# The second block's mixing stage: weight rounding, group sums and the first projection rows are put in another order

## The reference, cut to what matters

```python
y_f = _fourier_mix(zf, w_fourier[l])                       # 256 columns
q, k = _rope(zq, positions), _rope(zk, positions)
y_a = _window_attn(q, k, v, sink[l])                       # 8 heads of 64
y_m = _memory_attn(zm, km, vm)                             # 4 heads of 64
gg = g_grp[l]
y = jnp.concatenate([_rmsnorm(y_f, gg[:256]), _rmsnorm(y_a, gg[256:768]), _rmsnorm(y_m, gg[768:])], axis=-1) @ w_out[l]
x = x + _rmsnorm(y, g_post_mix[l])
```

## Time and profile before

| what | us |
|---|---|
| median of 3 runs | 1994.9 (1992.32 to 1998.2) |
| the profiled execution | 1989.49 |
| its span | 1987.6 |
| TensorE busy in it | 1834.7 (92%) |
| VectorE busy | 1252.5 (63%) |
| ScalarE busy | 850.6 (43%) |
| GpSimd busy | 302.4 (15%) |
| mean granted clock of TensorE | 0.972 of full |

### The profile page before, as it was taken

One profiled execution on the slowest core, in us unless ns is written; L12 is line 12 of the kernel. 1 busy time (PEld: TensorE's weight loads), 2 busy tenths in 40 slices (PEclk: granted clock), 3 DMA queues, 4 the chain that ended last, 5 costly groups with the idle time before them and its releaser, 6 DMA issues. The chain is left out here.

```text
span 1987.6 us, 42705 instructions
## 1 busy us (share of the span) xinstructions
PE 1834.7 (92%) x18268; PEld 1606.2 (81%) x18268; DVE 1252.5 (63%) x2177; ACT 850.6 (43%) x1561; POOL 302.4 (15%) x341
## 2 busy tenths in 40 slices
PE   7999868968999999999998899999889999889997
PEld 5787437858688888889877799999589999679997
DVE  4574886677656434534667778645768667677753
ACT  4321576363423212222436455533654355554332
POOL 0201206134140000013004101012040012030001
PEclk9999989979999999999999999999999999999998
DMA  9752940010523232323320455555045465226543
GB/s 326 210 175 85 311 135 3 15 53 2 170 85 106 85 106 85 106 85 94 119 64 1 152 168 175 186 191 170 1 150 190 143 196 174 82 86 194 188 156 99
DMA packets 248982, 254.69 MB, mean 128 GB/s; under 512 B 6914, under 2 KB 247186, under 8 KB 248690
## 3 DMA queue, kind: packets, MB, share of 16 engines
q1 hardware_dynamic: 239214, 242.86, 38.2%
q10 hardware_dynamic: 8740, 8.51, 1.3%
q0 software_dynamic: 864, 0.98, 0.3%
HBM read 251.29 MB, written 1.05 MB: 127 GB/s over the span
## 5 line engine op out<-in xcount | busy, mean ns | idle before, releaser
L578 DVE TENSOR_TENSOR RING_rounded<-RING,SC_rounded 128x1024 fp32r<-128x1024 f32 (+2 forms) x390 | 461.2, 1225 | 228.5 <-ACT SC_rounded L571 228.2
L598 PE MATMUL bank<-OT_rounded,SC_rounded 128*128 128x256 f32 (+1 forms) x1808 | 575.3, 318 | 15.5 <-DVE HT_rounded L1173 6.8
L600 PE MATMUL bank<-OT_rounded,RING_rounded 128*128 128x256 f32 (+1 forms) x1808 | 571.6, 316 | 0.0
L599 PE MATMUL bank<-HT_rounded,SC_rounded 128*128 128x256 f32 (+1 forms) x1808 | 570.3, 315 | 0.0
L571 ACT ACTIVATE SC_rounded<-RING 128x1024 fp32r<-128x1024 f32 (+2 forms) x390 | 373.8, 1009 | 331.5 <-DMA RING<-in_l_mlp_w 184.8
L598 PEld LDWEIGHTS bank<-OT_rounded,SC_rounded 128*128 128x128 f32 x1808 | 344.0, 190 | 44.7 <-issue 9.0
L600 PEld LDWEIGHTS bank<-OT_rounded,RING_rounded 128*128 128x128 f32 x1808 | 342.5, 189 | 23.8
L599 PEld LDWEIGHTS bank<-HT_rounded,SC_rounded 128*128 128x128 f32 x1808 | 342.3, 189 | 23.2
L598 PE MATMUL bank<-PT_rounded,SC_rounded 128*128 128x256 f32 (+1 forms) x896 | 277.4, 310 | 5.0 <-DVE RING_rounded L578 5.0
L600 PE MATMUL bank<-PT_rounded,RING_rounded 128*128 128x256 f32 (+1 forms) x896 | 277.5, 310 | 0.0
L599 PE MATMUL bank<-PT_rounded,SC_rounded 128*128 128x256 f32 (+1 forms) x896 | 277.1, 309 | 0.0
(11 more groups left out here) (573 smaller groups left out, 2782.4 us busy)
## 6 DMA issues: line engine op xcount, KB each, us to landing
RING<-in_l_mlp_w SPq DMA_DIRECT2D x64, 1024.0 KB, 5.3
RING<-in_w_ffn_in SPq DMA_DIRECT2D x44, 1024.0 KB, 5.1
RING<-in_l_mod_w SPq DMA_DIRECT2D x32, 1024.0 KB, 6.6
RING<-in_l_w_in SPq DMA_DIRECT2D x25, 1024.0 KB, 5.9
RING<-in_w_ffn_out SPq DMA_DIRECT2D x16, 768.0 KB, 4.8
RING<-in_w_in SPq DMA_DIRECT2D x10, 1024.0 KB, 5.3
RING<-in_w_ffn_out SPq DMA_DIRECT2D x16, 640.0 KB, 5.1
PT<-in_l_mod_w SPq DMA_DIRECT2D x8, 1024.0 KB, 10.1
```

Of the source, the lines that this page charges most:

```text
L578: net.nc.vector.tensor_tensor(low, whole, net.high4(s, m)[:, 0:self.w.kts[s], :].bitcast(F32), ALU.subtract).then_inc(self.split_ready, 1)
L598: net.nc.tensor.matmul(bank[:, tokens], high, x_high, start=start, stop=False)
L599: net.nc.tensor.matmul(bank[:, tokens], high, x_low, start=False, stop=False)
L600: return net.nc.tensor.matmul(bank[:, tokens], low, x_high, start=False, stop=stop)
```

## The change

On ScalarE the four high halves of slots 0 and 1 are now the first instructions of the stage. On VectorE the first low half comes ahead of the rotations' products, the other three behind them. TensorE sums groups 0 and 1 after pair 3's weighted values, in banks 0 and 1, and only group 2 behind the last pair; ScalarE takes roots 0 and 1 ahead of the last shares. VectorE scales tiles 0 and 1 before the last output, tiles 6 and 7 behind it, then makes four low halves, and only then scales by root 2. ScalarE's highs follow that: two before the last squares, two behind, then root 2, then four. Every instruction is kept; only order and two banks change. Line numbers are higher after the change, by 2 in ScalarE's part of the mixers, by 4 to 8 in VectorE's, and by up to some 25 further on.

```diff
-    def on_pe(self, pe):
+    def on_pe(self, pe, between={}):
...
             if pair:
                 weigh(pair - 1)
+            if pair in between:
+                between[pair]()
...
+            if u == self.N - 1:
+                share(self.N // 2 - 1)
             if u % 2 == 1 and u >= 5:
                 square(u // 2 - 2)
-        share(self.N // 2 - 1)
+        between[self.N]()
         square(self.N // 2 - 2)
         square(self.N // 2 - 1)
...
+        weights.low(dve, 0, 0)
         for n in range(4):
             part(n)
+        weights.low(dve, 0, 1)
+        for m in range(2):
+            weights.low(dve, 1, m)
         maxima(0)
...
-    group_banks = [net.ps[6][:, lats], net.ps[7][:, lats], net.ps[6][:, lats]]
+    group_banks = [net.ps[0][:, lats], net.ps[1][:, lats], net.ps[6][:, lats]]
...
+            def sum_first_groups():
+                pe.wait_ge(mixers.transform_taken, 6)
+                sum_group(0, 0)
+                sum_group(1, 1)
+
+            mixers.on_pe(pe, {4: sum_first_groups})
+            pe.wait_ge(mixers.out_taken, 5)
+            sum_group(2, 3)
+            pe.wait_ge(group_root, 2)
             rows_side_by_side(pe, out, 0, group_split, order)
...
-            mixers.on_act(act, {8: lambda: runner.highs(act, 0), 9: lambda: runner.highs(act, 1)})
-            for g in range(3):
-                root(g)
-            for n, t in enumerate(order):
-                act.wait_ge(group_scaled, n + 1)
-                act.activation(out.x.high[:, t], out.x.whole[:, t], ACT.Copy).then_inc(group_high, 1)
+            runner.highs(act, 0)
+            runner.highs(act, 1)
+            mixers.on_act(act, {10: first_roots, 12: lambda: high(0, 2)})
+            high(2, 2)
+            root(2)
+            high(4, 4)
...
-            mixers.on_dve(dve, link)
-            runner.lows(dve, 0)
-            mixers.last_outputs(dve)
-            runner.lows(dve, 1)
...
+            mixers.on_dve(dve, link, out)
+            scale(0)
+            scale(1)
+            mixers.last_outputs(dve)
+            scale(2)
+            scale(3)
+            for n in range(4):
+                low(n)
+            scale(4)
+            for n in range(4, KT):
+                if n + 1 < KT:
+                    scale(n + 1)
+                low(n)
```

More of the change, by code:

```diff
@@ L1867, in on_act, with on_dve @@
                 between[u]()
+            if u == self.N - 1:
+                share(self.N // 2 - 1)
             if u % 2 == 1 and u >= 5:
                 square(u // 2 - 2)
-        share(self.N // 2 - 1)
+        between[self.N]()
         square(self.N // 2 - 2)
         square(self.N // 2 - 1)
-    def on_dve(self, dve, link):
+    def on_dve(self, dve, link, weights):
         net, nc, mem = self.net, self.nc, self.mem
@@ L2021, in _, with sum_group @@
         def _(pe):
[L2022 to L2035, removed]
-                step.then_inc(group_summed, 1)
+            def sum_group(g, squared):
+                for n, t in enumerate(groups[g]):
+                    if g:
+                        pe.wait_ge(mixers.squared, squared + n)
+                    step = nc.tensor.matmul(group_banks[g], net.const(C_ONES), mixed.squares[t], start=(n == 0),
+                                            stop=(n == len(groups[g]) - 1))
+                step.then_inc(group_summed, 1)
+            def sum_first_groups():
[6 more added lines that the diff above has]
+            pe.wait_ge(group_root, 2)
             rows_side_by_side(pe, out, 0, group_split, order)
@@ L2075, in root, with high, first_roots @@
                 act.activation(group_roots[g], group_roots[g], ACT.Exp, scale=-0.5).then_inc(group_root, 1)
-            mixers.on_act(act, {8: lambda: runner.highs(act, 0), 9: lambda: runner.highs(act, 1)})
-            for g in range(3):
-                root(g)
-            for n, t in enumerate(order):
-                act.wait_ge(group_scaled, n + 1)
-                act.activation(out.x.high[:, t], out.x.whole[:, t], ACT.Copy).then_inc(group_high, 1)
+            def high(first, count):
+                for n in range(first, first + count):
+                    act.wait_ge(group_scaled, n + 1)
+                    act.activation(out.x.high[:, order[n]], out.x.whole[:, order[n]], ACT.Copy).then_inc(group_high, 1)
+            def first_roots():
+                root(0)
+                root(1)
+            runner.highs(act, 0)
[4 more added lines that the diff above has]
+            high(4, 4)
             for n, (part, q) in enumerate(runner.slots):
@@ L2143, in scale, with low @@
                                                ALU.mult, ALU.mult).then_inc(group_scaled, 1)
[L2145 to L2148, removed]
+            def low(n):
+                t = order[n]
                 dve.wait_ge(group_high, n + 1)
```

## The result

The changed kernel takes 1982.28 us, the median of five runs (1973.1 to 1985.16), against 1997.65 us for five runs of the kernel before (1992.32 to 1998.2). The ratio is 0.992, with a 95% interval of 0.9903 to 0.9937: faster, by 15.4 us between the medians. 1979.4 us with 15.5 us gained was forecast.

What follows compares the result with a forecast made beforehand. Bound: ScalarE's unrelated rounding, TensorE's half clock after it, then a serial chain from output to low half. Layer 0's 8.3 plus layer 1's 7.2 gave 15.5 us off 1994.9: 1979.4 us, range 1972 to 1988.

Steps and rivals of the forecast that it cites:

- Part 1: Before the last weighted values: moving four high halves to the stage's start brings those values 4.25 us earlier.
- the half clock: TensorE's slow stretch behind the 3.29 us gap, in the last pairs' work: some 1.3 us of the 4.25 won.
- Part 2: Behind the last pair: with low halves gone and sums early, projection starts about 1425.4, 8.4 us earlier in all.
- The fifth row tile: In the projection, the first tile needing the third root: ready 3.4 us early, so nothing is lost.
- Part 3: What the stage's start pays for the moved halves: 0.1 us in layer 0, 1.2 us in layer 1.
- B: Rival, stage start: hides nothing, all 4.6 us paid in both layers; 7.6 us gained, 1987.3; chance 0.10.
- C: Rival, tail: TensorE's clock falls anyway, projection's first 4 us at half clock, 2 us lost a layer; 1983.4; chance 0.08.
- D: Rival, tail: new order gains nothing, first low half late, projection keeps its 5.85 us; 1987.7; chance 0.08.
- E: Rival, projection: TensorE loses full clock in the tail and doesn't regain it; 7 us slower, 2002; chance 0.04.

Runs made afterwards that it cites:

- the filler matmuls: Kernel before with six unused fp32 matmuls put in TensorE's idle time ahead of pair 4's weighted values; stages 47.67 and 45.99 us (layers 0, 1).
- part 1 alone: Kernel before with only the weights' four high and four low halves moved to the stage's start, old tail order kept; stages 43.38 and 43.39 us.
- part 2 alone: Changed kernel with the weights' high and low halves back in their old places, new tail order kept; stages 47.77 and 45.96 us.

## Why the prediction was right

| step | forecast | measured |
|---|---|---|
| end of the last weighted values, from the stage's start, layer 0 | 38.6 | 38.55 |
| from there to L598 | 1.7 | 1.70 in both layers |
| the start's cost, layer 0 and 1 | 0.1, 1.2 | 0, 1.08 |
| L598, layer 0 and 1 | 40.4, 39.8 | 40.25, 39.66 |
| gained, layer 0 and 1 | 8.3, 7.2 | 8.47, 7.37 |
| time | 1979.4 | 1982.28 |

**Part 1** held: with the four roundings out of ScalarE's way the shares come in time. In layer 0 the last values end 4.32 us earlier (42.87 to 38.55), with nothing paid at the start; 4.25 was forecast. The two causes in it, the waiting and the half clock, were separated by the filler matmuls: 1.36 us is the clock, where the forecast took 1.3.

**Part 2** held in size and in its reason. The bound that it named, 5.85 us behind the last values, is what part 1 alone shows (5.84), and 1.70 is what is left of it: 4.15 us, as forecast. On top of part 1 it brings 3.73 us in layer 1 (43.39 to 39.66), since the sums and roots moved forward put the last values 0.42 us later (37.54 to 37.96); in layer 0 it brings 3.13, with the clock at the start against it. Of the 4.15, 1.24 is the overlap with the third root. The rest I put down mainly to the sums of groups 0 and 1 leaving the tail, where 4.14 us of sums became 1.99; that part was not tried alone. The fifth row tile is not waited for, as forecast.

What the forecast did not say is that the parts depend on each other. Its terms read as if each had its price; in layer 1 part 1 gives 3.64 us alone and part 2 1.07, 4.7 of the 7.37. The new tail order needs VectorE free of low halves.

**Part 3** held for layer 1: 1.08 us by the spread's start, of which one low half taken away brought 1.01 back; 1.2 was forecast. For layer 0 the number held and the reason was missed. The forecast took VectorE's 4.14 us of idle time as belonging to the layer; but TensorE's clock falls there (L1708 takes 2.54 us in layer 0, 1.97 in layer 1), and in the one profile without the fall layer 0 pays as layer 1 does. The fall is in both profiles compared, as in eleven of twelve, but nothing in the forecast provided for it: without it in either, layer 0 would gain some 7.4 us like layer 1 and not 8.47, an estimate from layer 1's rows. The low halves were well placed: 0.57 and 2.83 us more are paid where all four stand first.

**The rivals.** B (all 4.6 us paid) is excluded by the first maxima and by layer 1's 39.66. C, the clock falling in the new tail, did not happen: 1.00 in each stretch with pauses of up to 0.69 us. It did happen in part 2 alone, behind a wait of 1.89 us, so it was a real danger; the new tail has no wait of that length. The Trainium skill (page "TensorE: Matmul & The Clock Gate", section "A second HAM failure mode: psum-queue depth-cycling") says that short and frequent pauses between groups of matmuls make the clock swing between its levels. The changed kernel's tail of short pauses, with its clock of 1.00, does not bear that out; what more frequent ones would do, no run here shows. D, in which 5.85 us stay behind the last values, is excluded by the 1.70; a late first low half is seen only where the weights' low halves are in the tail. E needed a clock that stays down; in part 2 alone it was back at 1.00 from 1446 to 1450, and no profile shows it down for longer than that in the projection.

**Where the number was lucky.** The medians differ by 15.4 us and the stages by 15.84, but single runs scatter by 12 us, so agreement within 0.1 us of the forecast's 15.5 is chance; the stage lengths are what bears it out. The time itself came out 2.9 us above the forecast mainly because the forecast started from 1994.9, the median of three runs of the kernel before, and five runs give 1997.65. The spread that I allowed for, 5 us, was less than half of the 12.

## What to carry to other kernels

When a stall ends a chain that goes from engine to engine, look for work on those engines that does not belong to the chain and has an idle place elsewhere; here the new tail order brought 1.07 us while four roundings and four low halves stood in the tail, and 3.73 us once they had left it (layer 1). Try the parts alone before crediting them: an order that puts scales, highs and squares close together pays only on engines that are empty. And judge a change of this size by the length of its stage in the profile, which repeated to 0.01 us in the one repetition, while the ratio of whole times, out of six runs, was known to 0.0017, some 3.4 us. Look at the clock in that stage as well: where it falls by chance at the start a layer moves by 0.6 to 1.7 us, and where it falls just behind the stage the loss is in no stage length.

## What the runs showed of the hardware

**The run's time goes roughly with the clock, upstream of the change.** The five runs of the changed kernel order themselves exactly by mean granted clock: 1973.1 us at 0.974, 1977.43 at 0.970, 1982.28 at 0.968, 1983.35 at 0.967, 1985.16 at 0.965. In the six runs of its repetition this holds only roughly: 1970.14 at 0.973 is the fastest and 1982.81 at 0.968 the slowest, but 1977.53 stands at 0.968 too. No run here varies that clock alone. Over 12 profiles, whose instructions ahead of the stage are the same, the stage in layer 0 began between 1381.55 and 1394.65. One place of it, in the kernel before and then after:

```profile
1000.00:1120.00 120.00, 107.38 (x764) 90.75 (x762) 82.88 (x165) 58.00 (x123) 22.22 (x20) 0.94 0.09 27
```

```profile
1000.00:1120.00 120.00, 109.33 (x749) 92.88 (x748) 81.61 (x160) 55.52 (x118) 22.21 (x20) 0.91 0.09 27
```

In the same 120 us the same code does 764 and 749 matmul records at 0.94 and 0.91. What decides in which run the clock falls more often stays open.

**Which pauses were followed by a lower clock.** After idle times of TensorE of 3.29, 3.10 and 2.16 us the next stretch was at 0.57 to 0.64, so mostly at the lower of the two levels. After those of 0.48 to 1.06 us in the tails, 1.66 ahead of a spread, 1.54 and 1.55 at the start of layer 1, and 1.77 and 1.78 ahead of the projection, it was 1.00 each time. Between them it went both ways. The 1.89 us ahead of the projection was followed by a fall three times and by 1.00 once, as shown above. The 1.86 us at the start of layer 0 was followed by a fall in eleven of twelve profiles, as in the changed kernel,

```profile
1390.00:1394.00 4.00, 4.00 (x16) 3.41 (x15) 4.00 (x7) 3.70 (x7) 0.00 (x0) 0.61 1.09 365
```

and by none in part 1 alone, which has the same instructions there:

```profile
1386.50:1391.00 4.50, 4.43 (x24) 3.73 (x26) 3.37 (x6) 4.46 (x8) 0.00 (x0) 1.00 1.06 355
```

So after 1.86 or 1.89 us the fall came often and not always, and what decides it no run here shows. Filler matmuls that brought the 3.29 us down to 0.71 kept the clock.
